# An attention stage reordered: scores first on VectorE, transposes and value products behind later units

## The reference, cut to what matters

```python
q = q_all.reshape(B, S, 16, 192)                    # 128 plain columns, 64 rotary ones
q = concat([q[..., :128], rotary(q[..., 128:], positions)])
kv = einsum('bsr,rhe->bshe', rms_norm(kv_a[..., :512]), w_kv_b)   # 128 of k, 128 of v per head
k = concat([kv[..., :128], broadcast(rotary(kv_a[..., 512:]))])
s = where(causal, einsum('bqhd,bkhd->bhqk', q, k) * 192**-0.5, -inf)
a = einsum('bhqk,bkhd->bqhd', softmax(s), kv[..., 128:])
y_mla = einsum('bse,ed->bsd', a * silu(z_mla), w_mla_proj)
```

## Time and profile before

| | |
|---|---|
| median of three runs | 2763.93 us |
| profiled execution, its own time | 2764.27 us |
| its span, first to last instruction | 2762.4 us |
| mean granted TensorE clock | 0.968 |
| PE busy | 2613.7 us (95%) |
| DVE busy | 1889.3 us (68%) |
| ACT busy | 1101.7 us (40%) |
| POOL busy | 1131.4 us (41%) |
| chain that ended last: PE, DMA, POOL, DVE | 74%, 8%, 8%, 7% |

### The profile page before, as it was taken

How to read it: one execution, slowest core, us unless ns; L and a number is a source line. 1 busy time by engine, 2 the same in 40 slices (tenths; PEclk the granted TensorE clock), 3 DMA queues, 4 the chain that set the end, 5 groups by cost and what they waited for, 6 DMA issues and landing times.

```text
span 2762.4 us, 46307 instructions
## 1 busy us (share of the span) xinstructions
PE 2613.7 (95%) x20096; PEld 2345.3 (85%) x20096; DVE 1889.3 (68%) x2324; ACT 1101.7 (40%) x1311; POOL 1131.4 (41%) x612
## 2 busy tenths in 40 slices
PE   5689989999999999999999899999999999999997
PEld 2268877778999999999998889889988888888996
DVE  1248863378988888888897775676545884887554
ACT  1133422244434444344446443444444444444453
POOL 0293011014899999999981575762000000000001
PEclk7599999999999999999999999999999999999998
DMA  8967647775877777777765766775766665666664
GB/s 309 325 185 185 183 154 255 244 232 168 244 229 243 243 236 239 239 240 239 241 217 140 198 176 197 208 199 173 190 190 188 163 169 182 178 172 167 185 185 120
DMA packets 759178, 568.38 MB, mean 206 GB/s; under 512 B 46496, under 2 KB 645664, under 8 KB 758848
## 3 DMA queue, kind: packets, MB, share of 16 engines
q1 hardware_dynamic: 758976, 565.42, 69.6%
HBM read 563.29 MB, written 2.10 MB: 205 GB/s over the span
## 4 chain that ended last, share of the span: by engine, by line
PE 74%; DMA 8%; POOL 8%; DVE 7%; ACT 2%; issue 1%; SPq 1%; DVEq 0%; POOLq 0%
PE bank L786 20%; PE bank L789 10%; PE bank L769 5%; PE bank L770 5%; PE bank L773 5%; PE bank L753 5%; PE bank L755 5%; PE bank L754 5%; PE bank L1010 2%; DMA ada<-w_ada 2%; PE bank L742 2%; DMA ring<-w_in 2%; POOL prod L626 2%; DVE w_low L1771 2%; PE bank L824 2%; PE bank L823 2%
## 5 line engine op out<-in xcount | busy, mean ns | idle before, releaser
L1771 DVE TENSOR_TENSOR w_low<-ring,w_high 128x2048 fp32r<-128x2048 f32 x388 | 953.3, 2458 | 310.7 <-ACT w_high L1338 303.5
L1338 ACT ACTIVATE w_high<-ring 128x2048 fp32r<-128x2048 f32 x388 | 738.3, 1904 | 367.7 <-DMA ring<-w_in 125.1
L786 PE MATMUL bank<-acts,w_high 128*128 128x512 f32 (+1 forms) x2960 | 718.9, 395 | 12.2 <-DVE acts L1838 6.4
L786 PEld LDWEIGHTS bank<-acts,w_high 128*128 128x128 f32 (+1 forms) x2960 | 548.4, 190 | 124.2 <-DVE acts L1838 6.5
L789 PEld LDWEIGHTS bank<-acts,w_low 128*128 128x128 f32 (+1 forms) x2960 | 379.1, 191 | 15.5 <-DVE w_low L1771 0.9
L626 POOL TENSOR_SCALAR prod<-adf,cact 128x512 f32<-128x512 f32 x165 | 376.6, 2282 | 22.3 <-DMA adf<-w_ada 6.2
L789 PE MATMUL bank<-acts,w_low 128*128 128x256 f32 (+1 forms) x2960 | 384.1, 283 | 0.2 <-DVE w_low L1771 0.2
L769 PE MATMUL bank<-acts,w_high 128*128 128x256 f32 x1504 | 371.3, 286 | 0.0
L770 PE MATMUL bank<-acts,w_high 128*128 128x256 f32 x1504 | 369.5, 285 | 0.0
L640 POOL TENSOR_TENSOR sumf<-sqf 128x256 f32<-128x256 f32 x1 | 0.7, 742 | 782.2 <-ACT sqf L1752 782.2
L627 POOL TENSOR_TENSOR acc<-prod,acc 128x512 f32<-128x512 f32 x165 | 300.7, 1822 | 13.8
(11 more groups left out here) (463 smaller groups left out, 3710.7 us busy)
## 6 DMA issues: line engine op xcount, KB each, us to landing
ring<-w_in SPq DMA_DIRECT2D x182, 1024.0 KB, 5.8
ring<-w_up SPq DMA_DIRECT2D x88, 1024.0 KB, 5.8
ada<-w_ada SPq DMA_DIRECT2D x76, 1024.0 KB, 6.2
adf<-w_ada SPq DMA_DIRECT2D x44, 1024.0 KB, 7.9
ring<-w_down SPq DMA_DIRECT2D x44, 1024.0 KB, 6.3
ring<-w_out SPq DMA_DIRECT2D x16, 1024.0 KB, 5.8
adg<-w_ada SPq DMA_DIRECT2D x64, 256.0 KB, 5.5
ring<-w_mla SPq DMA_DIRECT2D x16, 1024.0 KB, 5.6
```

The lines of the kernel that those rows point to most:

```text
L786: pe.matmul(o, wh[:, j], both, start=j == 0, stop=False, skip_group_check=True)
L1338: act.activation(WH[s][:, 0:WIDE[n]], ring[s][:, 0:WIDE[n]], ACT.Copy).then_inc(high_done, 1)
L1771: v.tensor_tensor(WL[s][:, 0:WIDE[n]], ring[s][:, 0:WIDE[n]], f32(WH[s][:, 0:WIDE[n]]), ALU.subtract)\
```

## The change

On VectorE the scores' block moves from behind z0's gate to right behind the release of the scores; z0's addition stands between the scores and the scaling; the w_low of the next qr and z0's gate come after the scaling. ScalarE makes the exponentials of the scores before that of z0. The transposes (`turned`, now a helper) leave the turn's end: for turns 0 to 2 and 4 to 6 they stand behind the next turn's qr, and the value product moves from behind qr to behind q0. After turn 3 they stand behind the qr of turn 4 and right ahead of the value product; after turn 7 they stay behind z1 on TensorE. ScalarE's copies to PT follow the same places, and so stand behind the copies of the next qr. The whole diff:

```diff
--- before.py
+++ after.py
@@ -1198,6 +1198,12 @@
                     mm = pe.transpose(o[:, to:to + P], p[:, n * P:n * P + P], cc(C_ID))
                 return mm
 
+            def turned():
+
+                for h in range(2):
+                    pe.wait_ge(dve_to_pe, B.up("dve_to_pe"))
+                    x_done(turn(x_bank(4 + h), Pr[:, h, :]))
+
             def mixed():
 
                 o = x_bank(7)
@@ -1214,9 +1220,11 @@
                 for i in range(4):
                     if 4 * half + i != 4:
                         std(("mla", half, i, "qr"), 1)
-                        if i:
-                            mixed()
+                    if i:
+                        turned()
                     paired(("mla", half, i, "q0"), 2)
+                    if i:
+                        mixed()
                     paired(("mla", half, i, "q1"), 3)
                     if 4 * half + i in (3, 4, 6):
                         ada(acc_g[(3, 4, 6).index(4 * half + i) % 2])
@@ -1257,15 +1265,13 @@
                             if n == 1:
                                 x_done(mm)
                     paired(("mla", half, i, "z1"), 2)
-                    for h in range(2):
-
-                        pe.wait_ge(dve_to_pe, B.up("dve_to_pe"))
-                        x_done(turn(x_bank(4 + h), Pr[:, h, :]))
 
                 if half:
+                    turned()
                     paired(("gl", 0), 0)
                 else:
                     std(("mla", 1, 0, "qr"), 1)
+                    turned()
                 mixed()
                 pe.wait_ge(mix_ready, 4 * half + 3)
                 for k in range(8):
@@ -1608,6 +1614,12 @@
                     ins = act.activation(rsw[r + 32:r + 64, :], bank[1][r:r + 32, 0:T], ACT.Copy)
                 ins.then_inc(bank_free[1], 1)
 
+            def turned():
+
+                for h in range(2):
+                    xw()
+                    act.activation(PT[:, h, :], bank[4 + h][:, 0:384], ACT.Copy).then_inc(x_free[4 + h], 1)
+
             def mixed(i):
                 B.up("x_full")
                 from_dve()
@@ -1643,10 +1655,12 @@
                 for i in range(4):
                     if 4 * half + i != 4:
                         taken_qr(half, i)
-                        if i:
-                            mixed(i - 1)
+                    if i:
+                        turned()
                     unit("mla", half, i, "q0")
                     act.activation(qn[:, 0, :], bank[2][:, 0:T], ACT.Copy).then_inc(half_taken, 1)
+                    if i:
+                        mixed(i - 1)
                     unit("mla", half, i, "q1")
                     act.activation(qn[:, 1, :], bank[3][:, 0:T], ACT.Copy).then_inc(half_taken, 1)
                     unit("mla", half, i, "kvb")
@@ -1654,8 +1668,6 @@
                     act.activation(vv[:, :, :, :], bank[7][:, :], ACT.Copy).then_inc(x_free[7], 1)
                     unit("mla", half, i, "z0")
                     half_of(zs[:, 0, :], 1)
-                    summed(1, "mla", half, i, "z0")
-                    act.activation(ez[:, 0, :], zs[:, 0, :], ACT.Exp, scale=-1.0).then_inc(act_to_dve, 1)
                     for h in range(2):
                         B.up("x_full")
                         from_dve()
@@ -1663,19 +1675,20 @@
                                        accum_out=small[:, 4 * h + 2:4 * h + 3])
                         act.activation(Pr[:, h, T:384], Pr[:, h, T:384], ACT.Exp, bias=small[:, 4 * h + 1:4 * h + 2],
                                        accum_out=small[:, 4 * h + 3:4 * h + 4]).then_inc(act_to_dve, 1)
+                    summed(1, "mla", half, i, "z0")
+                    act.activation(ez[:, 0, :], zs[:, 0, :], ACT.Exp, scale=-1.0).then_inc(act_to_dve, 1)
                     unit("mla", half, i, "z1")
                     half_of(zs[:, 1, :], 2)
                     summed(2, "mla", half, i, "z1")
                     act.activation(ez[:, 1, :], zs[:, 1, :], ACT.Exp, scale=-1.0).then_inc(act_to_dve, 1)
-                    for h in range(2):
-                        xw()
-                        act.activation(PT[:, h, :], bank[4 + h][:, 0:384], ACT.Copy).then_inc(x_free[4 + h], 1)
 
                 if half:
+                    turned()
                     gate(0)
                     gate_opened(0)
                 else:
                     taken_qr(1, 0)
+                    turned()
                 mixed(3)
                 for k in range(8):
                     ahead(UNIT["proj", half, k] + 2)
@@ -2365,11 +2378,6 @@
                     raw_tile(0)
                     B.up("x_free7")
                     v.memset(small[:, 61:62], 0.0).then_inc(dve_to_pe, 1)
-                    ahead("mla", half, i, "z0")
-                    added(zs[:, 0, :], 1)
-                    from_act()
-                    opened(ez[:, 0, :])
-                    seq(v.tensor_tensor(zs[:, 0, :], zs[:, 0, :], ez[:, 0, :], ALU.mult))
                     for h in range(2):
                         xw()
                         p = Pr[:, h, :]
@@ -2380,6 +2388,7 @@
                         v.tensor_reduce(small[:, 4 * h:4 * h + 1], p[:, 0:T], AX.X, ALU.max, negate=True)
                         v.tensor_reduce(small[:, 4 * h + 1:4 * h + 2], p[:, T:384], AX.X, ALU.max, negate=True)\
                             .then_inc(dve_to_act, 1)
+                    added(zs[:, 0, :], 1)
                     for h in range(2):
                         from_act()
                         p = Pr[:, h, :]
@@ -2387,6 +2396,10 @@
                         v.tensor_scalar(p[:, 0:T], p[:, 0:T], small[:, 4 * h + 2:4 * h + 3], None, ALU.mult)
                         v.tensor_scalar(p[:, T:384], p[:, T:384], small[:, 4 * h + 3:4 * h + 4], None, ALU.mult)\
                             .then_inc(dve_to_pe, 1)
+                    ahead("mla", half, i, "z0")
+                    from_act()
+                    opened(ez[:, 0, :])
+                    seq(v.tensor_tensor(zs[:, 0, :], zs[:, 0, :], ez[:, 0, :], ALU.mult))
                     ahead("mla", half, i, "z1")
                     added(zs[:, 1, :], 2)
                     from_act()
```

## The result

The changed kernel took 2745.47 us (median of six runs, 2741.3 to 2757.35), the one before beside it 2764.75 us (six runs): a ratio of 0.9933, 95% interval 0.9913 to 0.9953, or 18 us less, give or take 6. Forecast were 2751 us, with 2740 to 2764 as the range. The profiled execution took 2746.02 us, its span 2744.2, 18.2 less than before.

A forecast was written before the change was run, and what follows sets the result against it. TensorE, 95% busy, was taken as the bound, with 18.9 us of waits ahead of the attention stage's transposes. The terms -22.7 + 5.0 + 1.7 + 0 + 2.8 gave -13.2 us, from 2764.27 to 2751 us; range 2740 to 2764.

The forecast's parts named there:

- The wait goes: Turns 1, 2, 4, 5, 6: TensorE's wait ahead of the probabilities' transposes vanishes with its clock loss, -22.7 us.
- What is late next: q0 waits for z1's addition to free bank 2: 1.0 us in five turns, +5.0, plus one lost clock stretch, +1.7.
- late landings: Loads for the next qr landing late delay ScalarE's exponentials and so VectorE's list: 0.6 us a turn.
- The collisions: GpSimd stretches the w_lows and short scalings in VectorE's list behind the scores: 0.9 us a turn.
- The first half's end: Behind turn 3: the value product waits nearly 6 us, but VectorE's list ends S + 22.4 against S + 22.0: net 0.
- The second half's end: Behind turn 7: gl 0's bank is freed 1.9 us later, with an even chance of a clock stretch: +2.8 us.
- the covered case: Rival, 20%: z1's addition is in time every turn and the halves' ends cost nothing: 2738 to 2742 us.
- collisions in full: Rival, 13%: every GpSimd meeting blocks VectorE's list, 5.1 us in turn 4; q0 late, +14 us, 2778 us.
- The moved stall: Rival, 17%: q0 waits 2.3 us for bank 2 and loses a clock stretch in five turns: 2764, or 2760 us.

The follow-up runs named there:

- second profile: Profile of the changed kernel run again unaltered, beside runs of the kernel before on the other chip: 2745.86 us, ratio 0.9948.
- turn 3 early: Changed kernel with turn 3's transposes right behind z1 and its PT copies ahead of ScalarE's wait for z1's sum: 2756.64 us, ratio 0.9959.
- the ends mended: Changed kernel with z1's addition sooner, turn 3's transposes and both PT copies early, turn 7's old score order, VectorE's lists at halves' ends reordered: 2739.04 us, ratio 0.9909.
- turn 7 in the old order: Changed kernel with the score order of before in turn 7 alone, on VectorE and ScalarE: 2746.05 us, ratio 0.9940.

## Why the prediction was right

*The wait goes, -22.7.* Right in kind and place: no wait ahead of transposes is left, and the scalings end at S + 4.2. The experiments add that both halves of the change do this, each alone (the moves but for 0.3 us).

*What is late next, +5.0 and +1.7.* The right wait, released by the right instruction, but mis-sized: 2.9 us (2.1 in the second profile) instead of 5.0, and no fall of the clock at all instead of one. Of the terms behind it, the 0.6 us a turn for late landings was wrong: in the profile after, landings cost VectorE's list nothing. Even in turn 1, where the split of the next qr begins at S - 0.6, ScalarE's first exponential begins only 0.14 us later than in the other turns, and the last scaling begins at S + 3.9 as in turn 2, where the split begins at S - 4.4. The collisions, put at 0.9, were 0.8 to 1.0 us in four turns and 2.4 in turn 1. Bank 2 was free at S + 12.3 in turns 2, 5 and 6, not S + 13.2. The five turns gained 19.6 us where I had 16.0; that is most of the 5 us by which the forecast was too small.

*The first half's end, 0.* Measured -0.6, with the wait ahead of the product at 4.8 us for nearly 6 and the 2.2 us behind it gone. One step of the count is too long: from the end of z1's addition to the end of its gate's product I took 3.5 us here and 3.15 at the second half's end, while the earlier trace rows give 3.13 (1548.71 to 1551.84); with that the list ends at S + 22.0, as before, and the net stays 0. That the late copies cost nothing there is shown by turn 3 early; that VectorE's list does, in part only, by the ends mended.

*The second half's end, +2.8.* Measured +3.3 (+4.5 in the second profile): 1.3 us more for the bank, 0.45 ahead of the product, the rest clock, for which I had taken an even chance. Its cause is shown by turn 7 in the old order.

*Sum.* -13.2 forecast, -18.2 in the profiled executions. Of the 5 us between, 3.6 are the five turns and 0.6 the first half's end, less 0.5 at the second's; 1.4 lie ahead of the stage and belong to no term; nothing in the runs ties them to the change. The median, 2745.47, lies just below the forecast's own 2746 to 2756 and above the covered case, 2738 to 2742. The last rival, collisions in full, is refuted by VectorE's rows: the worst turn lost 2.4 us to them, not 5.1, and in the meetings with w_low it was mostly GpSimd that waited. The moved stall is refuted too, since in each of the two profiles only one q0 wait passed 0.4 us (1.9 in turn 1, 1.2 in turn 4). The five turns, forecast at 38 to 39 us, took 38.6 to 40.3 from S to S. The prediction does not say that the score order was not needed: I had asked what the whole does, not which half does it.

## What to carry to other kernels

Where a result is late for its user, moving the user behind work that is there anyway can bring all that a reordering of the producer brings, as it did here; try each half alone before keeping both. An engine's list that starts at another engine's mark idles until it, and what it used to do in that time comes back behind the mark: count the list to the next buffer that it frees, above all at a loop's end, where the unit that would cover it is missing.

## What the runs showed of the hardware

That collisions fall in step was new to me: after the change the same operation (z0's product) was hit in turns 1 to 6 alike, at 1.34, 1.18, 1.18, 1.19, 1.18 and 1.19 us for 0.43. In turns 2 to 6 the step is set by VectorE's own long operation ahead of it: whenever GpSimd's multiplication began, at S + 4.3 to 5.9, it ended 1.6 us behind the end of w_low, and the addition behind it then stood in the product's way.

A wait of one length has no fixed price in clock. Over the 8 us behind the same wait of 3.4 us at gl 0 the mean granted clock was 0.79 in the changed kernel, 0.61 in its second profile, and 1.00 in the kernel without GpSimd's arithmetic.
